# RWKV-7 chunk inversion on 32x32 diagonal tiles, with VectorE block transposes, joined products and one table of decays

## What is computed

```python
def step(S, inp):
    r_t, w_t, k_t, v_t, a_t, b_t = inp          # a = -kk, b = kk * a_gate
    sa = jnp.einsum('bhij,bhj->bhi', S, a_t)
    S = S * w_t[:, :, None, :] + sa[..., None] * b_t[:, :, None, :] + v_t[..., None] * k_t[:, :, None, :]
    return S, jnp.einsum('bhij,bhj->bhi', S, r_t)
```

## Time and profile before

| | |
|---|---|
| three runs | 1957.57, 1960.16, 1960.64 us; median 1960.16 |
| the profiled execution | 1964.18 us, of which its span is 1962.6 us |
| busy share of the span | PE 97%, PEld 92%, DVE 58%, ACT 36%, POOL 9% |
| mean granted TensorE clock | 0.982 |
| first inversion round (L849) of the 8 pair steps | 463.15, 518.08, 572.95, 627.77, 682.59, 737.46, 792.32, 847.07 us |

### The profile page before, as it was taken

How to read it: one execution, slowest core, us unless ns; L and a number is a source line. 1 busy time by engine, 2 the same in 40 slices (tenths; PEclk the granted TensorE clock), 3 DMA queues, 4 the chain that set the end, 5 groups by cost and what they waited for, 6 DMA issues and landing times.

```text
span 1962.6 us, 40819 instructions
## 1 busy us (share of the span) xinstructions
PE 1894.2 (97%) x16568; PEld 1804.3 (92%) x16568; DVE 1139.6 (58%) x1983; ACT 715.0 (36%) x942; POOL 168.2 (9%) x126
## 2 busy tenths in 40 slices
PE   5999889999999999999999999999999999999997
PEld 3999769998888888889999999999999999999997
DVE  4333956226777776667655566666666666444444
ACT  4333243433443333334344333333333333333332
POOL 2600325441000000000000000000000000000000
PEclk7999989889999999999999999999999999999999
DMA  4644323431222222225444544444444444644443
GB/s 182 214 169 165 114 78 115 138 113 63 100 101 82 99 100 80 97 75 215 155 169 156 204 169 169 154 168 164 158 169 170 155 167 151 215 166 162 162 162 136
DMA packets 50746, 283.61 MB, mean 145 GB/s; under 512 B 7104, under 2 KB 12160, under 8 KB 24576
## 3 DMA queue, kind: packets, MB, share of 16 engines
q1 hardware_dynamic: 43488, 261.00, 39.0%
q10 hardware_dynamic: 3072, 12.63, 1.7%
q0 software_dynamic: 4128, 9.18, 1.3%
HBM read 274.51 MB, written 8.27 MB: 144 GB/s over the span
## 4 chain that ended last, share of the span: by engine, by line
PE 83%; DVE 10%; ACT 2%; issue 2%; DMA 1%; POOL 1%; DVEq 0%; ACTq 0%; SPq 0%
PE bank L561 25%; PE bank L563 23%; PE bank L562 23%; PE bank L849 3%; DVE w_lo L510 1%; PE bank L888 1%; POOL w_lo L510 1%; DVE w_lo L518 1%; DVE squares_k L1731 1%; DVE x_raw L1533 1%; DVE rkv L1688 1%; DVE rope_tmp L1571 1%; ACT w_hi L526 1%; DMA conv_params<-in_conv_params 1%; PE bank L702 1%
## 5 line engine op out<-in xcount | busy, mean ns | idle before, releaser
L561 PE MATMUL bank<-x_split,w_lo 128*128 128x288 f32 x2944 | 907.4, 308 | 25.5 <-DVE x_split L1539 16.7
L562 PE MATMUL bank<-x_split,w_hi 128*128 128x288 f32 x2944 | 873.5, 297 | 0.0
L563 PE MATMUL bank<-x_split,w_hi 128*128 128x288 f32 x2944 | 870.6, 296 | 0.0
L526 ACT ACTIVATE w_hi<-w_raw 128x2048 fp32r<-128x2048 f32 (+1 forms) x264 | 472.6, 1790 | 574.4 <-PE bank L563 561.7
L510 DVE TENSOR_TENSOR w_lo<-w_raw,w_hi 128x2048 fp32r<-128x2048 f32 (+1 forms) x215 | 451.2, 2099 | 310.6 <-ACT w_hi L526 310.6
L561 PEld LDWEIGHTS bank<-x_split,w_lo 128*128 128x128 f32 x2944 | 556.2, 189 | 52.9 <-issue 30.2
L562 PEld LDWEIGHTS bank<-x_split,w_hi 128*128 128x128 f32 x2944 | 558.0, 190 | 4.2 <-issue 0.7
L563 PEld LDWEIGHTS bank<-x_split,w_hi 128*128 128x128 f32 x2944 | 559.1, 190 | 0.0
L561 PE MATMUL bank<-act_split,w_lo 128*128 128x288 f32 x704 | 208.6, 296 | 0.5 <-DVE w_lo L510 0.5
L562 PE MATMUL bank<-act_split,w_hi 128*128 128x288 f32 x704 | 207.7, 295 | 0.0
L563 PE MATMUL bank<-act_split,w_hi 128*128 128x288 f32 x704 | 207.0, 294 | 0.0
(11 more groups left out here) (366 smaller groups left out, 1723.5 us busy)
## 6 DMA issues: line engine op xcount, KB each, us to landing
w_raw<-in_w_up SPq DMA_DIRECT2D x88, 1024.0 KB, 4.9
w_raw<-in_w_in SPq DMA_DIRECT2D x48, 1024.0 KB, 4.9
w_raw<-in_w_down SPq DMA_DIRECT2D x64, 704.0 KB, 4.1
w_raw<-in_w_gate SPq DMA_DIRECT2D x32, 1024.0 KB, 4.9
w_raw<-in_w_p SPq DMA_DIRECT2D x16, 1024.0 KB, 4.9
w_raw<-in_w_o SPq DMA_DIRECT2D x16, 1024.0 KB, 4.9
x_raw<-in_x SPq DMA_DIRECT2D x4, 576.0 KB, 6.7
h<-in_x ACTq DMA_DIRECT2D x1, 2304.0 KB, 10.2
```

Of the source, the lines that this page charges most:

```text
L526: actv(WHI[:, slot, 0:kt], WRAW[:, slot, 0:kt], ACT.Copy).then_inc(sem("w_hi"), 1)
L561: mm(out, wl, hi, start=first and k == ks[0], stop=False, skip_group_check=True)
L562: mm(out, w, lo, start=False, stop=False, skip_group_check=True)
L563: ins = mm(out, w, hi, start=False, stop=last and k == ks[-1], skip_group_check=True)
```

## The change

The inversion works on 32x32 diagonal tiles: four units of four 32x32 blocks (one for each quarter of the partitions) instead of 64x64 matrices that are zero outside their 16x16 blocks. `blockwise` makes 16 products, on the four diagonal 32x32 tiles of the array. The lower triangle is no longer multiplied out: DVE's `transpose` (32x32 blocks) makes it from the upper one. `U` and `T` lie side by side, so that one product with 64 columns gives the square and the product with T. The second merge takes only the 32x32 blocks that are not zero. L834 becomes half as wide (`LO`), L841 goes; `b_mm` makes only the diagonal 32x32 blocks of B^T A, and the rest in two further groups. The decays come from one table whose chunks have a leading column of zeros (65 columns for each chunk, 5 for each request), so that the exclusive sums are the same table shifted by one: 3 products instead of 6, two exponentials instead of three.

The core of the diff:

```diff
-    c["m16u"] = packed(blk(16) & up)
-    c["m16l"] = packed(blk(16) & low)
-    c["m32l"] = packed(blk(32) & ~blk(16) & low)
-    c["m64l"] = packed(blk(64) & ~blk(32) & low)
+    c["eye_bl"] = packed32(eye)
+    c["m16u"] = packed32(blk(16) & up)
+    c["m32u"] = packed32(blk(32) & ~blk(16) & up)
...
-                for bank, tri, tris in ((7, tri_incl, tris_incl), (2, tri_excl, tris_excl)):
-                    for tt in range(2):
-                        mm(BK[bank][:, tt * P:(tt + 1) * P], LDT[:, tt, :], tri, start=True, stop=True)
-                    ins = mm(BK[bank][:, SEQ:N], LDT[0:NS, 2, :], tris, start=True, stop=True)
-                ins.then_inc(sem("log_decay"), 1)
+                for tt in range(2):
+                    w = 2 * (CH + 1)
+                    mm(BK[7][:, tt * w:(tt + 1) * w], LDT[:, tt, :], tri, start=True, stop=True)
+                mm(BK[7][:, NCH * (CH + 1):DEC], LDT[0:NS, 2, :], tri_s, start=True, stop=True).then_inc(sem("log_decay"), 1)
...
-                for x, src in enumerate((BT, KTL)):
-                    for tt, par in chunks:
-                        c0 = (2 * tt + par) * CH
-                        for e, h in enumerate(halves):
-                            ins = mm(BK[5 + e][halves[par], x * SEQ + tt * P:x * SEQ + (tt + 1) * P], src[h, c0:c0 + CH],
-                                     AR[h, :, c0:c0 + CH], start=True, stop=True)
+                for tt, par in chunks:
+                    for b in range(2):
+                        c0, q = (2 * tt + par) * CH + b * BL, slice((2 * par + b) * BL, (2 * par + b + 1) * BL)
+                        for e, h in enumerate(halves):
+                            mm(BK[5 + e][q, tt * P:tt * P + BL], BT[h, c0:c0 + BL], AR[h, 0, c0:c0 + BL], start=True, stop=True)
...
+                        mm(BK[5 + e][halves[par], tt * P + CH:(tt + 1) * P], BT[h, c0:c0 + CH], AR[h, 1, c0:c0 + CH],
+                           start=True, stop=True)
...
+                        ins = mm(BK[5 + e][halves[par], SEQ + tt * P:SEQ + (tt + 1) * P], KTL[h, c0:c0 + CH],
+                                 AR[h, :, c0:c0 + CH], start=True, stop=True)
...
-                        mm(BK[(4, 7)[e]][halves[par], tt * CH:(tt + 1) * CH], AR[h, 0, c0:c0 + CH], BT[h, c0:c0 + CH],
+                        mm(BK[(4, 7)[e]][halves[par], tt * BL:(tt + 1) * BL], AR[h, 0, c0:c0 + CH], BT[h, c0:c0 + BL],
...
-                    mm(out[:, 2 * P:2 * P + NS], ARS[h, 0, :], BKS[h, 0, :], start=True, stop=True)
...
+                def blockwise(bank, lhs, rhs, both=False):
+                    w = 2 * BL if both else BL
                     for u in range(4):
-                        for r in halves:
-                            ins = mm(BK[bank][r, c0 + u * CH:c0 + (u + 1) * CH], lhs[r, u], rhs[r, u], start=True, stop=True)
+                        for q in quads:
+                            ins = mm(BK[bank][q, u * w:(u + 1) * w], lhs[q, u], rhs[q, u], start=True, stop=True)
+                    ins.then_inc(sem("inv_mm"), 1)
...
-                four(2, 0, L1, U1)
-                four(3, 0, U1, L1).then_inc(sem("inv_mm"), 1)
+                blockwise(2, L1, U)
                 fill(2)
-                pe.wait_ge(sem("inv_u"), v * 5 - 4)
                 pe.wait_ge(sem("inv_l"), v * 8 - 7)
                 settle(pe)
-                four(2, 0, L2, U2)
-                four(3, 0, U2, L2)
-                four(3, 256, L2, TT).then_inc(sem("inv_mm"), 1)
+                blockwise(3, L2, UT, True)
                 fill(3)
...
-                four(2, 0, U1, L1)
-                four(3, 256, L1, TT).then_inc(sem("inv_mm"), 1)
+                blockwise(2, L1, UT, True)
...
-                four(3, 0, L2, TT).then_inc(sem("inv_mm"), 1)
+                blockwise(3, L2, T)
...
-                    for u in range(4):
-                        for r in halves:
-                            mm(BK[2][r, u * CH:(u + 1) * CH], TT[r, u], ident[r, r], start=True, stop=True)
-                    four(3, 256, U1, TT).then_inc(sem("inv_mm"), 1)
+                    if merge == 0:
+                        blockwise(2, LB, T)
+                    else:
+                        for u in range(4):
+                            for g in (1, 3):
+                                ins = mm(BK[2][quads[g - 1], u * BL:(u + 1) * BL], LO[quads[g], u // 2, u % 2 * BL:(u % 2 + 1) * BL],
+                                         T[quads[g], u], start=True, stop=True)
+                        ins.then_inc(sem("inv_mm"), 1)
...
-                        four(3, 0, L1, L2).then_inc(sem("inv_mm"), 1)
+                        blockwise(3, L1, L2)
...
-                        four(3, 0, L1, L2).then_inc(sem("inv_mm"), 1)
+                        for u in range(4):
+                            for g in (0, 2):
+                                ins = mm(BK[3][quads[g], u * BL:(u + 1) * BL], L1[quads[g], u], L2[quads[g], u], start=True,
+                                         stop=True)
+                        ins.then_inc(sem("inv_mm"), 1)
```

On ACT the third exponential, three of the five copies of a round's result (`evac`) and the wait for `block16` go. DVE's part:

```diff
-                    ins = V.tensor_tensor(U1[:, 2 * e:2 * e + 2, :], src[:, 0:2, 0:CH], spread(m16u, 1, [P, 2, CH]), ALU.mult)
+                    src = BK[5 + e][:, 0:2 * P].rearrange("p (u f) -> p u f", u=2)[:, :, 0:BL]
+                    ins = V.tensor_tensor(U[:, 2 * e:2 * e + 2], src, spread(m16u, 1, [P, 2, BL]), ALU.mult)
                 st.done(ins)
-                V.tensor_tensor(TT[:], U1[:], spread(eye_ch, 1, [P, 4, CH]), ALU.add)
-                dve.wait_ge(sem("k_mm"), v)
+                V.transpose(L1[:], U).then_inc(sem("block16"), 1)
+                st.mark(V.tensor_tensor(T, U, spread(eye_bl, 1, [P, 4, BL]), ALU.add))
                 for e in range(2):
-                    ins = V.tensor_tensor(L1[:, 2 * e:2 * e + 2, :], grid((4, 7)[e], 0, 2), spread(m16l, 1, [P, 2, CH]), ALU.mult)
-                ins.then_inc(sem("block16"), 1)
+                    src = BK[5 + e][:, 0:2 * P].rearrange("p (u f) -> p u f", u=2)[:, :, 0:BL]
+                    ins = V.tensor_tensor(UB[:, 2 * e:2 * e + 2, :], src, spread(m32u, 1, [P, 2, BL]), ALU.mult)
+                st.done(ins)
...
                 inv(1)
-                V.tensor_copy(L2[:], grid(3, 0)).then_inc(sem("inv_l"), 1)
+                V.transpose(L2[:], blocks(2))
+                V.tensor_copy(U, blocks(2)).then_inc(sem("inv_l"), 1)
+                V.transpose(LB[:], UB[:])
...
                 inv(2)
-                V.tensor_copy(L1[:], grid(3, 0))
-                add_t(3, 256, 2)
+                u, t = parts(3)
+                V.transpose(L1[:], u)
+                V.tensor_copy(U, u)
+                add_t(t, 2)
...
-                    V.tensor_tensor(MLS[:, e, :], src[:, 2 * P:2 * P + NS], ms_l, ALU.mult)
-                st.mark(ins)
-                st.sync()
+                st.done(ins)
+                V.transpose(MLS[:], MBKS[:, :, 0:NS])
...
                 inv(3)
-                add_t(3, 256, 3)
-                V.tensor_tensor(U1[:], ML[:], spread(m32l, 1, [P, 4, CH]), ALU.mult)
+                u, t = parts(2)
+                V.transpose(L2[:], u)
+                add_t(t, 3)
...
                 inv(4)
-                add_t(3, 0, 4)
+                add_t(blocks(3), 4)
+                V.transpose(L1[:], T).then_inc(sem("inv_l"), 1)
...
                 inv(6)
-                add_t(3, 0, 6)
+                add_t(blocks(3), 6)
+                V.transpose(L1[:], T).then_inc(sem("inv_l"), 1)
+                st.mark(V.tensor_tensor(TT[:].rearrange("p u (k f) -> p u k f", k=2), spread(T, 2, [P, 4, 2, BL]),
+                                        spread(own_block, 1, [P, 4, 2, BL]), ALU.mult))
...
                 inv(8)
-                add_t(3, 0, 8)
+                st.sync()
+                for q in (slice(0, BL), slice(2 * BL, 3 * BL)):
+                    ins = V.tensor_copy(TT[q, :, BL:CH], BK[3][q, 0:4 * BL].rearrange("p (u f) -> p u f", u=4))
+                ins.then_inc(sem("inv_l"), 1)
```

More of the change, by code:

```diff
@@ L58 @@
 CH = 64
+BL = 32
 NCH = SEQ // CH
+DEC = NCH * (CH + 1) + DB * (DS + 1)
 KEYS_S = PAST + DS
@@ L90, in constants, with packed32 @@
     c["head_ones"] = blk(HD)
-    c["tri_incl"] = (blk(CH) & upi) * (0.5 * DECAY_SCALE)
-    c["tri_excl"] = (blk(CH) & up) * (0.5 * DECAY_SCALE)
     def packed(m):
         return np.concatenate([m[0:CH, 0:CH], m[CH:P, CH:P]], 0)
+    tri = np.zeros((P, 2, CH + 1))
+    tri[:, :, 1:] = ((blk(CH) & upi) * (0.5 * DECAY_SCALE)).reshape(P, 2, CH)
+    c["tri"] = tri.reshape(P, -1)
     c["eye_ch"] = packed(eye)
     c["m_ab"] = np.concatenate([packed(up), packed(upi)], 1)
-    c["m16u"] = packed(blk(16) & up)
-    c["m16l"] = packed(blk(16) & low)
-    c["m32l"] = packed(blk(32) & ~blk(16) & low)
-    c["m64l"] = packed(blk(64) & ~blk(32) & low)
+    def packed32(m):
+        return np.concatenate([m[g:g + BL, g:g + BL] for g in range(0, P, BL)], 0)
+    c["eye_bl"] = packed32(eye)
+    c["m16u"] = packed32(blk(16) & up)
```

(27 more changed lines are left out.)

90 lines of the change are left out of this document (43 added, 47 removed).

## The result

The kernel after takes 1928.41 us (median; 1924.94 to 1929.12) against 1960.4 us (1957.57 to 1961.12) for the kernel before in the same comparison: ratio 0.9832, interval 0.9819 to 0.9845. The forecast was 1930.4 us, range 1921 to 1948.

A forecast was written before the change was run, and what follows sets the result against it. PE was taken to bound the inversion rounds, DVE the stretch behind the last state. Savings of 1.75 and 1.97 us made 3.7 a pair step, 29.8 in all, from 1960.2 to 1930.4 us; range 1921 to 1948.

The forecast's parts named there:

- What bounds the kernel: PE bounds from the first inversion round to W and U; DVE from the last state to the next first round.
- The rounds: Inversion and merges on PE: 0.40 us a round with 32 columns, 0.59 with 64; together 3.58 us in place of 7.56.
- Rivals 2 and 3: Every round and `b_mm`: records stay 30 ns apart, 1966 us, chance 0.06; or have a 25 ns floor, 1956 us, 0.04.
- What lay behind the state products: The later rounds, round 4 and the merges, pay in full because DVE and ACT have idle time: 1.97 us a pair.
- The waits on DVE: PE waits for DVE 0.1 us ahead of round 2, 0.1 ahead of round 3, 0.35 ahead of the state products.
- `b_mm`: More, smaller records behind the split: +0.1 us, given back by L834 and L841 (-0.1); bounds 0 and +0.8.
- `log_decay` at nothing: Behind the last state, 3 products instead of 6 take 0.97 us less on PE, gaining nothing because DVE sets that stretch.
- rival 5: PE's longer wait behind `kk_sum` lowers its clock to 1.2 GHz: 1.7 us at each of seven boundaries, 1942 us; chance 0.06.
- The sum: A pair step saves 3.7 us, the first 3.9; 29.8 us in all, for a median of 1930.4 us.

The follow-up runs named there:

- e12: The kernel after with later quarter splits, with round 4 and the first merge's first round making every product twice: 1929.45 us, ratio 0.9846 to the kernel before.
- e2: The kernel before with the shifted decay table alone (3 products in `log_decay`, two exponentials), inversion unchanged: 1961.24 us, ratio 1.0000 to the kernel before.
- e10: The kernel after with `log_decay`'s three products made twice: 1931.19 us, ratio 0.9854 to the kernel before.
- e5: The kernel after with the 32x32 tiles one after the other instead of in turn, same products: 1962.77 us, ratio 1.0007 to the kernel before.
- e3: The kernel after with DVE's four quarter splits moved later, behind the operands of rounds 2 and 3: 1922.69 us, ratio 0.9808 to the kernel before.
- e7: The kernel after with the five early block transposes made twice on DVE: 1943.51 us, ratio 0.9911 to the kernel before.
- e9: The kernel after with 96 always-met waits (48 instructions a pair) ahead of the bonus product: 1950.46 us, ratio 0.9954 to the kernel before.
- e8: The kernel after with later quarter splits, with round 4 and the first merge's two rounds making every product twice: 1954.35 us, ratio 0.9963 to the kernel before.
- e6: The kernel after with every product of the six full rounds of 32 records made twice: 1973.31 us, ratio 1.0059 to the kernel before.
- e4: The kernel after with square and product with T taken apart, 64 records of 32 columns in rounds 2 and 3: 1931.94 us, ratio 0.9844 to the kernel before.
- e11: The kernel after with 400 always-met waits (200 instructions a pair) ahead of the bonus product: 2091.73 us, ratio 1.0677 to the kernel before.

## Why the prediction was right, step by step

**What bounds the kernel: right.** PE bounds the rounds (e12: 0.63 in, 0.63 out), DVE the stretch from the last state to its split (e2 and e10: 0.97 and 0.66 us of PE's work removed and added, the pair step did not move). Behind the split PE's own work counts again, which the prediction passed over; see `b_mm`.

**The rounds: right.** 0.38 and 0.58 us for 0.40 and 0.59. The argument that each tile has its own pace and tiles run beside each other was tested by e5: without the turns between tiles the same records take more than twice as long. But the pace was mis-sized. A tile by itself has its records 23 ns apart, not 40, and four tiles in turn bring 8.4 ns, 2.7 times as fast and not four times. 40 / 4 and 23 / 2.7 lie close together: the two errors cancelled, which was luck. Rivals 2 and 3 fall with the 8.4 ns. The rule of about 25 ns in "TensorE: Matmul & The Clock Gate" of the Trainium skill, section "Wait — 56ns, not 53.3ns?", is near what e5 shows for a tile by itself (23 ns), and is not a floor for tiles in turn.

**What lay behind the state products: too low.** I had 1.97 us a pair, the timelines give 0.36 (round 4), 0.70, 0.36 (first merge), 0.71, 0.24 (second) = 2.37. Of the 0.40, 0.30 come from round 4 and the merge's second round: a small product in the same 32x32 shape follows there (L921, L953), and it starts 0.01 us behind the start of the last record, where I had booked 0.12 for leaving the tile shape. The other 0.10 comes from rounds of 0.37 or 0.38 us, where I had 0.40.

**The waits on DVE: right in place, off in size.** Ahead of round 2 the fill is 0.39 longer than one without a wait (0.1 predicted), ahead of round 3 0.08 (0.1), ahead of the state products 0.26 (0.35). Together 0.73 in place of 0.55. Counted from the start of DVE's first product (509.23; 516.63 before), round 2's operands are there after 2.81 us (2.67 predicted: transposes that hold the queue 0.24 in place of 0.20, and their neighbours), and PE could be there after 1.05 + 0.38 + 0.99 = 2.42 (2.58 predicted: PE reaches round 1 0.13 earlier). Counted from the start of its fill, round 1 came 0.30 us earlier (0.27 predicted), and the state products came 1.63 us earlier, not 1.75. e3 shows that the order of the queue was the cause: with the splits moved all three waits are gone.

**`b_mm`: slightly wrong.** It was booked at nothing and gave 0.13 us. Its 32 records of 64x32 need 0.28 us to the next start (557.93 to 558.21), 9 ns each, not 16.

**`log_decay` at nothing: right** (e2, e10). **The clock (rival 5): did not come** in the kernel after, although PE waits 0.79 us there; but it came in variants that wait or crawl more in the rounds (e5, e7) and, with 1.9 us more of waiting, at the very place that rival 5 named (e9: six of seven pair steps, some 1.5 us each, near the 1.7 that it was priced at).

**The sum.** 1.63 + 2.37 + 0.13, less 0.04 for a longer group of state products, are 4.1 us; 4.05 measured; 3.7 predicted. Eight times 0.35 are 2.8 us, of which 2.0 show in the median. The forecast hit nearly what came, by terms that were off by up to 0.4 us a pair, in both directions: the mechanism was right, that the sum came so near was in part luck.

## What to carry to other kernels

When PE's small products shrink, look at once at what DVE has queued ahead of the next operand: moving the quarter splits behind the third round was worth 6 us here, a fifth of the whole change. Put small products on different array tiles in turn, and follow them by work in the same tile shape. And read the packets of the instruction queue in every variant of a loop: a "what if" kernel with doubled work can lose 24 us (e8) or 34 us (e6) to loading its own program and the half clock that came with it, which says nothing about the work.

## What the runs showed of the hardware

**A loop body has a length from which it is loaded anew.** With 128 instructions more a pair than in the kernel after, 42 packets (e4, e12); with 192, 200 and 384 more, 97, 97 and 98 (e8, e11, e6). The growth is 8 packets a pass, (1.61 - 0.67) MB / 57 = 16.5 KB each. In e6 and e8 PE then stops for 1.1 to 1.7 us at the loop's start and 1.3 to 2.9 us ahead of L856, in each pass from the second on, and its clock can be at half close to that. In e11, with as many packets, the stops are 0.4 to 1.7 us, at the loop's start alone. "Runtime: NRT & Kernel Launch" of the Trainium skill, section "Instruction fetch mechanics", says that instructions are loaded in blocks of 16 KiB (256 instructions), that PE's memory for them holds 2048, and that a taken branch to a target outside the window that is held stops the engine until the page is fetched. The size of the packets agrees, and eight blocks are 2048 instructions. No run here counts the instructions of the loop body itself, so the limit is bracketed only as growth.

**Tiles.** Four 32x32 tiles in turn take a record each 8.4 ns (32 columns) or 14 ns (64); one tile after the other 23 and 38 ns (e5).

**The change of tile shape.** From the start of a round's last record to a product of the same tile shape 0.01 us, to a fill 0.12 (0.38 - 0.26).

**A 32x32 block transpose on DVE** of 128x128 fp32 takes 0.31 us, from SBUF or from PSUM, and 0.23 us for 32x64.

**Half clock in small-tile rounds.** In e7 it followed PE busy for 3.29 of 4 us in one pair step, and did not follow the same 3.29 of 4 at the same place of a later one in the same execution. In e5 it followed PE busy for 4.00 of 4. So PE's busy time there does not tell them apart, and what does stays open; so does the spell in e4's first pair step.
